# Opening of a two-block transformer kernel: later load of the column constants, one weight split moved behind the token split, two clears moved behind the gates

## The reference, cut to what matters

```python
h = _layer_norm(jnp.concatenate([meta, x], axis=1), ln0_g, ln0_b)
...
    p = h @ w_in[layer] + b_in[layer]
    u_s5, q, k, v, o_pre, i_pre, f_pre, g_s5, g_m = _split_columns(p)
    y_s5 = _s5_mixer(u_s5, s5_lambda_re[layer], s5_lambda_im[layer], s5_log_dt[layer],
                     s5_b_re[layer], s5_b_im[layer], s5_c_re[layer], s5_c_im[layer], s5_d[layer])
```

## Time and profile before

| | us |
|---|---|
| median of 3 runs | 748.54 |
| lowest, highest | 748.45, 749.19 |
| the profiled execution | 748.5 |
| its span on the core | 746.7 |
| TensorE busy in the span | 729.2 |
| VectorE busy | 585.9 |
| ScalarE busy | 467.8 |
| GpSimd busy | 144.8 |

### The profile page before, as it was taken

The page is one execution under the profiler, slowest core; times in us unless marked ns, Lnnn a source line. Parts: engine busy times, 40 slices in busy tenths (PEclk is TensorE's granted clock), DMA queues, the critical chain, the costliest instruction groups (busy, mean ns, idle before and its releaser), DMA issues.

```text
span 746.7 us, 14448 instructions
## 1 busy us (share of the span) xinstructions
PE 729.2 (98%) x5355; PEld 672.6 (90%) x5355; DVE 585.9 (78%) x868; ACT 467.8 (63%) x789; POOL 144.8 (19%) x143
## 2 busy tenths in 40 slices
PE   7999999999999999999999999999999999999996
PEld 7899999999999798998889888997889999999995
DVE  7997989844976577776686998988788888866667
ACT  7768775669765475455554539668676555555565
POOL 6000000001234023323232330010003212343330
PEclk9999999999999999999999999999999999999999
DMA  8455433155555849988787882942237775565551
GB/s 303 141 173 169 149 126 137 65 151 178 177 180 171 312 146 408 319 307 316 229 281 255 272 323 73 358 178 95 92 104 232 248 246 184 185 194 190 179 170 57
DMA packets 47314, 150.68 MB, mean 202 GB/s; under 512 B 9472, under 2 KB 10888, under 8 KB 47256
## 3 DMA queue, kind: packets, MB, share of 16 engines
q1 hardware_dynamic: 45272, 145.86, 58.0%
q10 hardware_dynamic: 1984, 4.03, 1.6%
HBM read 147.73 MB, written 1.06 MB: 199 GB/s over the span
## 4 chain that ended last, share of the span: by engine, by line
PE 87%; DVE 5%; ACT 4%; issue 2%; DMA 1%; SPq 0%; ACTq 0%; DVEq 0%
PE ps L823 32%; PE ps L764 21%; PE ps L511 18%; PE ps L1066 2%; PE ps L1126 1%; ACT wh L1181 1%; PE ps L525 1%; PE ps L529 1%; DVE wl L1769 1%; PE ps L526 1%; PE ps L618 1%; PE ps L1007 1%; DMA vtk<-in_x 1%; PE ps L544 1%; PE ps L637 1%
## 5 line engine op out<-in xcount | busy, mean ns | idle before, releaser
L1769 DVE TENSOR_TENSOR wl<-raw,wh 128x1024 fp32r<-128x1024 f32 x220 | 283.6, 1295 | 88.2 <-ACT wh L1181 86.7
L1181 ACT ACTIVATE wh<-raw 128x1024 fp32r<-128x1024 f32 x220 | 231.5, 1054 | 68.1 <-PE ps L764 49.5
L823 PE MATMUL ps<-xh,wh 128*128 128x256 f32 x672 | 189.8, 282 | 0.5 <-ACT zv L1632 0.5
L823 PE MATMUL ps<-xh,wl 128*128 128x256 f32 x672 | 188.3, 280 | 0.0
L823 PE MATMUL ps<-xl,wh 128*128 128x256 f32 x672 | 188.2, 280 | 0.0
L823 PEld LDWEIGHTS ps<-xh,wh 128*128 128x128 f32 x672 | 126.6, 188 | 4.9 <-issue 2.1
L823 PEld LDWEIGHTS ps<-xl,wh 128*128 128x128 f32 x672 | 126.6, 188 | 1.9
L823 PEld LDWEIGHTS ps<-xh,wl 128*128 128x128 f32 x672 | 126.7, 189 | 0.0
L511 PE MATMUL ps<-xh,wh 128*128 128x256 f32 (+2 forms) x400 | 117.2, 293 | 1.9 <-DVE wl L1769 0.8
L511 PE MATMUL ps<-xh,wl 128*128 128x256 f32 (+2 forms) x400 | 113.2, 283 | 0.0
L511 PE MATMUL ps<-xl,wh 128*128 128x256 f32 (+2 forms) x400 | 113.0, 283 | 0.0
(11 more groups left out here) (422 smaller groups left out, 1241.9 us busy)
## 6 DMA issues: line engine op xcount, KB each, us to landing
raw<-in_w_stream SPq DMA_DIRECT2D x220, 512.0 KB, 4.1
ada_w<-in_w_ada SPq DMA_DIRECT2D x48, 512.0 KB, 6.0
vtk<-in_x SPq DMA_DIRECT2D x2, 512.0 KB, 5.8
tg_m<-in_ln_rows ACTq DMA_DIRECT2D x2, 512.0 KB, 6.9
out<-ob SPq DMA_DIRECT2D x4, 256.0 KB, 2.0
u<-uT SPq DMA_DIRECT2D x16, 34.0 KB, 2.4
eepp<-in_s_mats SPq DMA_DIRECT2D x1, 512.0 KB
decay_rows<-decay_dram SPq DMA_DIRECT2D x4, 128.0 KB
```

The costliest lines, as they stand in the source:

```text
L823: mm = nc.tensor.matmul(ps[:, bank, 0:SEQ], w, x, start=(k == 0), stop=(k == 3 * KD - 1))
L1181: nc.scalar.activation(wh[:, b % RING], raw[:, b % RING], ACT.Identity).then_inc(hi_done, 1)
L1769: V.tensor_tensor(wl[:, b % RING], raw[:, b % RING], wh[:, b % RING].bitcast(F32), ALU.subtract).then_inc(lo_done, 1)
```

## The change

Four things are done. The scale and shift of the first norm move to the front of the table `cols`, so that the first piece that ScalarE loads has 128 columns (64 KB) and holds them; the other 439 columns are loaded by SyncE behind block 3, and ScalarE waits for them only ahead of the first copy of a block out of PSUM. On VectorE `lo(1)` stands behind the split of the tiles. On TensorE `first_blocks` gives way, for blocks 0 and 1, to `opening_blocks`: five products for each tile, and the eight that need the low part of block 1 at the end; block 0 is signalled as done ahead of these. On GpSimd the clears of `vtk` and `eepp` wait for the gate products.

```diff
@@ the table
-    for name, n in (("lam_re", 16), ("lam_im", 16), ("log_dt", 16), ("power", 64), ("b_in", 44), ("conv_w", 32), ("conv_b", 8), ("s5_d", 16), ("ln0_g", 8), ("ln0_b", 8),
+    for name, n in (("lam_re", 16), ("lam_im", 16), ("log_dt", 16), ("power", 64), ("ln0_g", 8), ("ln0_b", 8), ("b_in", 44), ("conv_w", 32), ("conv_b", 8), ("s5_d", 16),
...
-NLAM = 112
+NLAM = 128
@@ SyncE
+            sp.dma_start(cols[:, NLAM:NCOL], A["cols"][:, NLAM:NCOL]).then_inc(S["cols_landed"], 16)
             sp.dma_start(s5m[:, :, :, :], A["s5_mats"]).then_inc(S["gates_landed"], 16)
@@ TensorE
+            def opening_blocks():
...
+                pe.wait_ge(*lo_made(B_U))
+                pe.wait_ge(hi_done, B_U + 2)
+                for m in range(KD):
+                    pe.wait_ge(*ln("ln0", "hi", m + 1))
+                    nc.tensor.matmul(bank[0], weight(wh, 0, m), xh[:, m, :], start=(m == 0), stop=False)
+                    nc.tensor.matmul(bank[0], weight(wl, 0, m), xh[:, m, :], start=False, stop=False)
+                    nc.tensor.matmul(bank[1], weight(wh, 1, m), xh[:, m, :], start=(m == 0), stop=False)
+                    pe.wait_ge(*ln("ln0", "lo", m + 1))
+                    mm = nc.tensor.matmul(bank[0], weight(wh, 0, m), xl[:, m, :], start=False, stop=(m == KD - 1))
+                    if m == KD - 1:
+                        mm.then_inc(blk_done, 1)
+                    nc.tensor.matmul(bank[1], weight(wh, 1, m), xl[:, m, :], start=False, stop=False)
+                pe.wait_ge(*lo_made(B_U + 1))
+                for m in range(KD):
+                    mm = nc.tensor.matmul(bank[1], weight(wl, 1, m), xh[:, m, :], start=False, stop=(m == KD - 1))
+                mm.then_inc(blk_done, 1)
...
-            first_blocks(B_U, (0, 1), "ln0", 0)
+            opening_blocks()
@@ ScalarE
-            act.dma_start(cols[:, NLAM:NCOL], A["cols"][:, NLAM:NCOL]).then_inc(S["cols_landed"], 16)
...
             hi(1)
-            act.wait_ge(S["cols_landed"], 16)
...
+                if b == B_U:
+                    act.wait_ge(S["cols_landed"], 16)
@@ VectorE
             lo(0)
+            split("ln0", res, 0)
             lo(1)
-            split("ln0", res, 0)
@@ GpSimd
             G.memset(vtk[:, :, :, DV:DV + 1], 1.0).then_inc(pool_step, 1)
+            pool.wait_ge(S["gate_mm"], 1)
             G.memset(vtk[:, 0, :, 0:DV], 0.0).then_inc(S["c_cleared"], 1)
```

More of the change, by code:

```diff
@@ L513, in product, with weight @@
                 return mm
+            def opening_blocks():
+                bank = [ps[:, n, 0:TOK] for n in range(2)]
+                def weight(w, n, m):
+                    return w[:, n, m * P:(m + 1) * P]
+                pe.wait_ge(*lo_made(B_U))
[14 more added lines that the diff above has]
+                mm.then_inc(blk_done, 1)
             def first_blocks(b, banks, tag, first=META):
```

## The result

| | before | changed |
|---|---|---|
| median, us (22 runs each) | 748.76 | 750.26 |
| lowest to highest | 747.53 to 750.15 | 747.73 to 752.54 |
| ratio to before, 95% interval | | 1.0018 [1.0012, 1.0024] |
| first profiled execution, and its span | 748.5, 746.7 | 750.84, 749.1 |

The medians lie 1.50 us apart; by the ratio the change costs 1.35 us, with an interval of 0.9 to 1.8. That is 0.18% of the time, small but clear of the noise. The forecast was a gain of 0.34 with a range up to 749.5: the sign is wrong and the time lies outside the range.

A forecast was written before the change was run, and what follows sets the result against it. VectorE's queue was taken to set block 7's start. Gains of 0.30 there and 0.26 from `x`, less 0.27 for a held cast, plus about 0.05, gave 0.34: 748.5 us to 748.2, range 747.7 to 749.5.

The forecast's parts named there:

- Columns later: Loading most of `cols` behind block 3 lets `x` land and be scaled earlier: 0.26 us, between 0 and 0.53.
- `lo(1)` behind the split: VectorE's first cast starts 0.61 us earlier, but a third subtraction of 1.135 follows the split: costs 0.52 us.
- two clears later: Moving GpSimd's clears of `vtk` and `eepp` takes 0.83 us of a held cast out of VectorE's split.
- the clear that stays: GpSimd's clear of `hraw` now meets VectorE's first cast and holds it: 0.27 us lost.
- The sum up to `lo(7)`: VectorE's queue comes 0.29 us earlier, with about 0.05 more behind `phases`, so block 7 starts 0.34 earlier.
- Order of the products: On TensorE the 0.46 us gap ahead of block 2 goes; block 7's gap takes it back, becoming 1.15 us.
- Clears at the gates: Gate products end 0.7 to 0.9 us earlier; VectorE's `TENSOR_SCALAR` passes about 0.3 ahead of the clears; cost nothing.
- The clears catch VectorE: Rival: the clears hold VectorE in `eigenvalues`, 1.28 us on the chain to `lo(7)`, giving 749.4; chance 0.1.
- The clock falls at block 7: Rival: the longer gap ahead of block 7 halves TensorE's clock, costing 1.7 us, giving 749.9; chance 0.1.
- The row from which I argued: Profile row: after TensorE's 1.3 us wait at the transposes, its granted clock stood at 0.50.
- I carry the shift to the end.: Behind block 7 both engines are shifted alike, so the 0.34 us gained there reaches the kernel's end.

The follow-up runs named there:

- r1: The kernel before, unedited, profiled a second time; span 745.4 us.
- e2: The changed kernel with its clears of `vtk` and `eepp` waiting for `lo(6)` in place of the gate products; ratio to before 1.0000.
- e5: The kernel before with the later load of the columns and the clears of `vtk` and `eepp` behind `lo(6)`; ratio 0.9987.
- e3: The changed kernel with the clears of `vtk` and `eepp` early, where the kernel before has them; ratio to before 1.0005.
- e4: The changed kernel with seven identity products into an unused bank ahead of block 7 on TensorE; ratio to before 1.0015.
- e7: The changed kernel with block 0 signalled as done one product ahead of the end of block 1, not nine; ratio to before 1.0003.
- e11: The kernel before with only the new order on TensorE and VectorE, columns and clears as before; ratio 1.0010.
- e6: The kernel before with only the clears of `vtk` and `eepp` waiting for the gate products; ratio 0.9995.

## Why the prediction was wrong, step by step

*Columns later.* The sign is right, the size is not: 0.26, at most 0.53, against 0.50 to 0.65 in the mean of the profiles and 1.52 between the first two. The first profile of before had its `x` 1.21 later than r1, the latest of all six. I took one execution's landing time for the kernel's.

*`lo(1)` behind the split, two clears later, the clear that stays.* These held. Three subtractions follow the split, no cast of 1.13 is left (worth 0.71 instead of the 0.83 of my sum), and the first cast took 0.69 instead of 0.30, held by the clear of `hraw` as forecast; I had priced that at 0.27, it is 0.39. With the meeting at the gates taken away (e2) block 7 starts 0.15 to 0.19 us earlier behind `x`; my terms without `x` gave 0.34 - 0.26 = 0.08. The sum up to `lo(7)` was right to about 0.1, apart from `x`.

*Order of the products.* The gap ahead of block 2 went, and block 7 took it back. I forecast a gap of 1.15 us; without the meeting it is 1.67 (e2). Nothing was late of what I had named (`lo(1)`, block 5, the columns).

*Clears at the gates.* This is the step that failed. I had the gate products end "some 0.7 to 0.9 earlier", of which 0.26 was `x`, and the `TENSOR_SCALAR` pass "ahead of them by some 0.3 us". By the table the gate products end 19.01 us behind `x` before and 17.93 after: 1.08 earlier, not 0.44 to 0.64. I had given TensorE the net gain of VectorE's queue, in which the returned third subtraction eats what the unheld casts give. But that subtraction stands behind what TensorE needs, so TensorE keeps the full 0.7 (19.10 in r1 against 18.39 in e5), and the gap of 0.46 on top (17.93). VectorE has that 0.7 less the returned subtraction. So the small operation, which passed 0.81 ahead of the end of the gate products in the profile from which I predicted and 0.94 ahead in r1, came 0.10 behind it, while I had left 0.3. The cost that I put at nothing was 0.98 us. The same slip made the gap of block 7 too small.

*The rivals.* "The clears catch VectorE" was the case, and came in all five profiles that have the new order, the early signal and the clears at the gates; its price of up to 1.28 was near (1.04 on the row, 0.98 at block 7). "The clock falls at block 7" was the case too; its price of 1.7 was good (1.5), its condition was not: the clock stayed behind all gaps of 1.08 to 1.68 (e2, e3, e4, e7, e11). The row from which I argued was no rule either: in e6 TensorE waits 1.45 us at the same transposes, and neither the column nor the durations show a lower clock. I treated the two as independent tenths, and gave both together 0.05. They are one chain: the catch lengthens the gap by what it costs VectorE, and the clock fell behind the longer gap alone, in three of the four profiles that have it.

*"I carry the shift to the end."* This failed too. TensorE is 0.78 us late at block 8 and 0.64 at 163 us, but 2.3 behind the long stretch, a term that my sum didn't have.

*How much each is worth.* For the same landing of `x`, the held operation costs 1.0 at block 7, shown by e2 and e7. The lower clock adds 1.5 in the profiles in which it falls, shown by e4. The long stretch adds 1.5 to 2, its cause open. The timed executions show 1.35 in all, less than the profiles' sum, since `x` gives some of it back and since not every execution has every loss. e7 suggests that the held operation and the clock together make up most of the 1.35, since it lacks only these and lies at 1.0003; a finer division the intervals don't allow.

## What to carry to other kernels

When work is reordered, move each engine by its own queue: a net sum over one engine doesn't hold for another that needs only the first part of it, and the distance between two engines can close though both gain. A GpSimd clear that is placed by another engine's event can come to lie on a VectorE operation that it holds, however small that is; place it by VectorE's own progress, behind an operation of which one knows what follows (here `lo(6)`). And before a few tenths are forecast from one profile, look how much its first loads scatter from one execution to the next.
